# Low parts of the rotated queries and keys in retention: made by GpSimd in place of the vector engine

## The reference

```python
q = rotary(q.reshape(B, S, H, RET_QK), positions)
k = rotary(k.reshape(B, S, H, RET_QK), positions) * (RET_QK ** -0.5)
def step(R, chunk):
    qc, kc, vc = chunk
    inner = jnp.einsum('bhqk,bhkd->bhqd', jnp.einsum('bhqd,bhkd->bhqk', qc, kc) * decay_in[None], vc)
    cross = jnp.einsum('bhqd,bhde->bhqe', qc, R) * xi[None, :, :, None]
    R = R * gamma_c[None, :, None, None] + jnp.einsum('bhkd,bhke->bhde', kc * zeta[None, :, :, None], vc)
    return R, inner + cross
```

## Time and profile before

| | |
|---|---|
| time, median of 3 runs | 1608.7 us (1607.95 to 1609.33) |
| the profiled execution, its own time | 1608.6 us |
| span, first to last instruction | 1606.8 us |
| mean granted PE clock | 0.995 |

### The profile page before, as it was taken

How to read it: one execution, slowest core, us unless ns; L and a number is a source line. 1 busy time by engine, 2 the same in 40 slices (tenths; PEclk the granted TensorE clock), 3 DMA queues, 4 the chain that set the end, 5 groups by cost and what they waited for, 6 DMA issues and landing times. The chain is left out here.

```text
span 1606.8 us, 20289 instructions
## 1 busy us (share of the span) xinstructions
PE 1565.4 (97%) x7568; PEld 1306.9 (81%) x7568; DVE 960.0 (60%) x1626; ACT 605.1 (38%) x1057; POOL 323.7 (20%) x280
## 2 busy tenths in 40 slices
PE   5999999999999999999999999999999999999998
PEld 4778888888888888788888888887688888888886
DVE  6984444444444448752665666667978775647544
ACT  5443333333333353342343333434544444213111
POOL 2232222333232200200000000025545530000000
PEclk8999999999999999999999999999999999999999
DMA  9133233323333234699364464548977767344332
GB/s 385 41 120 116 105 112 111 111 106 112 110 125 107 92 107 157 263 414 341 122 210 158 167 213 166 175 143 278 322 227 226 252 208 274 113 149 179 136 105 79
DMA packets 142225, 278.70 MB, mean 173 GB/s; under 512 B 11056, under 2 KB 83632, under 8 KB 133552
## 3 DMA queue, kind: packets, MB, share of 16 engines
q1 hardware_dynamic: 125488, 245.09, 43.9%
q10 hardware_dynamic: 12032, 15.54, 2.9%
q0 software_dynamic: 4608, 16.78, 2.6%
HBM read 182.47 MB, written 94.37 MB: 172 GB/s over the span
## 5 line engine op out<-in xcount | busy, mean ns | idle before, releaser
L1586 DVE TENSOR_TENSOR w_form<-w_pair,w_form 128x512 fp32r<-128x512 f32 x150 | 116.3, 777 | 127.2 <-ACT w_form L1218 125.6
L1218 ACT ACTIVATE w_form<-w_pair 128x512 fp32r<-128x512 f32 x150 | 94.6, 632 | 245.2 <-PE p_banks L2100 237.2
L2097 PE MATMUL p_banks<-h_hi,w_form 128*128 128x512 f32 x300 | 116.8, 389 | 1.1 <-DVE w_form L1586 1.1
L2100 PE MATMUL p_banks<-h_hi,w_form 128*128 128x512 f32 x300 | 116.7, 389 | 0.0
L2099 PE MATMUL p_banks<-h_lo,w_form 128*128 128x512 f32 x300 | 116.7, 389 | 0.0
L1290 ACT ACTIVATE prob<-p_banks,neg_max 128x128 f32<-128x128 f32 (+3 forms) x64 | 47.5, 742 | 183.0 <-DVE neg_max L1700 183.0
L529 ACT ACTIVATE w_hi<-w_raw 128x1024 fp32r<-128x1024 f32 (+3 forms) x63 | 53.1, 847 | 135.8 <-PE p_banks L2355 97.9
L2355 PE MATMUL p_banks<-y_hi,w_lo 128*128 128x512 f32 x256 | 99.6, 389 | 0.0
L2354 PE MATMUL p_banks<-y_lo,w_hi 128*128 128x512 f32 x256 | 99.6, 389 | 0.0
L2353 PE MATMUL p_banks<-y_hi,w_hi 128*128 128x512 f32 x256 | 99.6, 389 | 0.0
L1062 POOL DMA_DIRECT2D v_ret<-v_stage x32 | 17.7, 554 | 399.2 <-DVE v_stage L1677 399.1
(11 more groups left out here) (318 smaller groups left out, 4313.9 us busy)
## 6 DMA issues: line engine op xcount, KB each, us to landing
w_pair<-in_w_pairs SPq DMA_DIRECT2D x25, 1024.0 KB, 4.8
w_raw<-in_w_dense SPq DMA_DIRECT2D x39, 512.0 KB, 4.7
v_ret<-v_stage POOLq DMA_DIRECT2D x32, 512.0 KB, 3.3
v_chunk<-v_ret SPq DMA_DIRECT2D x32, 512.0 KB, 3.8
merge_t<-act_t SPq DMA_DIRECT2D x48, 256.0 KB, 3.4
act_t<-stage SPq DMA_DIRECT2D x40, 256.0 KB, 2.0
act_t<-stage_late SPq DMA_DIRECT2D x40, 256.0 KB, 2.0
ada<-in_w_ada SPq DMA_DIRECT2D x4, 2048.0 KB, 23.8
```

The costliest lines, as they stand in the source:

```text
L1218: self.nc.scalar.activation(self.form[f % FORM_SLOTS][:, 0, :], self.form_source(f), ACT.Copy).then_inc(self.form_hi, 1)
L1586: nc.vector.tensor_tensor(self.form[f % FORM_SLOTS][:, 1, :], self.form_source(f), self.form[f % FORM_SLOTS][:, 0, :].bitcast(F32), ALU.su ...
L2097: self.nc.tensor.matmul(out, w_hi[:, cut], x_hi[:, q, :], start=fresh and q == 0, stop=False, skip_group_check=True)
L2100: last = self.nc.tensor.matmul(out, w_lo[:, cut], x_hi[:, q, :], start=False, stop=q == KD // 2 - 1, skip_group_check=True)
```

## The change

`low_qk` is issued on POOL in place of DVE: the same subtraction, of the same operands into the same place, behind the same wait for ACT's high part, and counted in the same semaphore. On DVE the three calls go. On POOL, `low_qk(n)` stands directly behind the rotation of chunk n for n from 2 on; `low_qk(0)` comes at g = 64 and `low_qk(1)` at g = 66, both behind the rotations of chunks 0 and 1. Buffers and all other work stay.

```diff
--- before.py
+++ after.py
@@ -1029,11 +1029,16 @@
             if g == STEPS - 2:
                 for n in range(2):
                     self.rotate_chunk(pool, n)
+            if g == STEPS:
+                self.low_qk(pool, 0)
+            if g == STEPS + 2:
+                self.low_qk(pool, 1)
         for n in range(2, CHUNK_STEPS):
             if n == 9:
                 for unit in range(units, FILL_UNITS):
                     self.store_fill(pool, unit)
             self.rotate_chunk(pool, n)
+            self.low_qk(pool, n)
 
     def rotate_chunk(self, pool, n):
 
@@ -1332,9 +1337,9 @@
             act.wait_ge(self.out_done, n - 1)
         self.nc.scalar.activation(self.qk[:, n % 2, 0:4, :], self.qk_raw[n % 3][:, 0:4, :], ACT.Copy).then_inc(self.qk_hi_ready, 1)
 
-    def low_qk(self, dve, n):
-        dve.wait_ge(self.qk_hi_ready, n + 1)
-        self.nc.vector.tensor_tensor(self.qk[:, n % 2, 4:8, :], self.qk_raw[n % 3][:, 0:4, :],
+    def low_qk(self, pool, n):
+        pool.wait_ge(self.qk_hi_ready, n + 1)
+        self.nc.gpsimd.tensor_tensor(self.qk[:, n % 2, 4:8, :], self.qk_raw[n % 3][:, 0:4, :],
                                      self.qk[:, n % 2, 0:4, :].bitcast(F32), ALU.subtract).then_inc(self.qk_lo_ready, 1)
 
     def high_chunk(self, act, n):
@@ -1735,11 +1740,8 @@
             while parts < self.parts_used(g - 1):
                 self.lower_weight(dve, R_V + V_PARTS + parts)
                 parts += 1
-            if g == STEPS - 1:
-                self.low_qk(dve, 0)
             if g == STEPS + 1:
                 self.low_chunk(dve, 0)
-                self.low_qk(dve, 1)
 
     def merge_unit(self, dve, unit):
 
@@ -1824,8 +1826,6 @@
                 dve.wait_ge(self.yr_stored[s], 16 * (n // 2))
             nc.vector.tensor_tensor(self.y_ret[:, s, :, :], p[:, 0, :].rearrange("p (a n) -> p a n", n=P),
                                     self.gate_chunk[:, n % 3, :, :], ALU.mult).then_inc(self.yr_done, 1)
-            if n + 2 < CHUNK_STEPS:
-                self.low_qk(dve, n + 2)
             if n == len(FILL_LATE) - 1:
                 for unit in range(FILL_UNITS - 2, FILL_UNITS):
                     self.lower_fill(dve, unit)
```

## The result

| | before | after |
|---|---|---|
| time, median (lowest to highest) of 20 runs each | 1606.95 us (1605.45 to 1609.33) | 1610.62 us (1609.25 to 1612.90) |
| ratio, 95% interval | | 1.0023 [1.0017, 1.0030] |
| span of the profiled execution | 1606.8 us | 1609.0 us |

The change costs 3.7 us (interval 2.7 to 4.8, the ratio's ends times 1607). The forecast was 1614.2, +5.6 on the profiled execution; 1610.62 lies in the range. The three runs known when the forecast was made had a median 1.75 us above that of the 20, so part of its distance from the result lies in its starting point.

A forecast was written before the change was run, and what follows sets the result against it. The prediction took PE, busy 97% of the span, as the bound, with DVE mattering only where PE waits for it. Terms 2.0 - 1.6 + 3.0 + 1.4 + 0.8 = +5.6 on 1608.6 gave 1614.2 us, range 1609.5 to 1618.5.

The forecast's parts named there:

- the first rival: Chunks 4 and 5: POOL doesn't get between two successive DVE instructions; each loses 0.35; +3.3 us, 1611.9; chance 0.18.
- Term 1: Head of retention: PE stands still for POOL's subtraction of chunk 0, queued behind two rotations; +2.0 us.
- Term 2: Chunks 0 and 3, where DVE was late on its own: the splits end earlier, 1.0 and 0.6; -1.6 us.
- so I see no cover: Head: nothing later hides PE's 2.0 us stop, as all hangs on PE or a load behind it.
- Term 3: Chunks 4 and 5: POOL's subtraction and a rotation product take turns with DVE's splits, 1.5 us each; +3.0 us.
- neither is stretched: Kernel before: POOL's rotation runs while DVE reads PSUM, so neither engine slows the other; no size given.
- Term 4: Chunks 6 to 8: chunk 9's rotation, behind two stores, ends late, delaying ACT and chunk 8's statistics; +1.4 us.
- Term 5: Later chunks: one POOL turn delays w_lo ahead of the statistics, 0.64 in chunk 15, 0.2 in chunk 22; +0.8 us.
- The clock: PE's slow stretch from 1108.4 to 1111.8 us: one lost and one gained cancel; 0, between -1.6 and +3.2 us.
- The Trainium skill's other rule: DVE and POOL sharing SBUF: DVE instructions with one SBUF input don't contend; no size given.
- The second: From 1085 to 1165 us: DVE's relief reaches PE, waits and slow clock go; -6.3 us, 1602.3; chance 0.07.
- The third: POOL's chain per chunk, 8.6 against 7.5 us, becomes the bound; some ten chunks late; +5 on top, 1619; chance 0.13.

The follow-up runs named there:

- Experiment 2: The changed kernel with chunk 0's subtraction put between the head's two rotations on POOL: 1608.23 us, 1.0012 of the kernel before.
- experiment 9: The kernel before with only chunk 0's subtraction moved to POOL, between the head's two rotations: 1605.26 us, ratio 0.9986.
- the repeat: The kernel before, timed and profiled once more without an edit: 1606.63 us, ratio 1.0002.
- Experiment 4: The changed kernel with the rotations of chunks 7, 8 and 9 held until DVE's splits are made: 1609.11 us, 1.0017 of the kernel before.
- experiment 5: The kernel before with only the subtractions of chunks 6, 7 and 8 moved to POOL: 1612.42 us, ratio 1.0033.
- 6: The kernel before with only the subtractions of chunks 2 and 5 moved to POOL: 1606.73 us, ratio 0.9998.
- 7: The kernel before with only the subtractions of chunks 0 and 1 moved to POOL, behind both head rotations: 1608.24 us, ratio 1.0004.
- 8: The changed kernel, all 32 subtractions on POOL but several re-placed among the rotations, chunk 9's rotation held: 1605.90 us, 0.9994 of the kernel before.
- 10: The kernel before with the subtractions of chunks 0 to 3 moved to POOL, chunk 0's between the head's rotations: 1605.37 us, ratio 0.9985.
- experiment 3: The changed kernel with each subtraction from chunk 3 on behind the next chunk's rotation: 1608.61 us, 1.0017 of the kernel before.

## Why the prediction was right, and where it was off

The direction and the mechanism hold; the sum was 5.6 us for 3.7 measured, and 4.7 by the waits of the two profiles. Of the 3.6 us between 1614.2 and 1610.62, 1.65 is the execution that the forecast started from (1608.6 for a median of 1606.95), and 1.9 the sum. By the time alone the first rival, at +3.3, comes nearer than the forecast; the trace is what decides for the forecast. By its own steps:

- **Term 1, the head: 1.67 for 2.0**. The subtraction took 1.26 us and the rotation ended a little sooner than taken. Experiment 2 shows that the order costs it: without it 1.8 us are gone.
- **Term 2, chunks 0 and 3: 2.1 gained for 1.6.** Chunk 0 gave 1.85 for 1.0, and here a step failed: "Everything later hangs on PE's fills, on the load of chunk 2 behind them, or on PE itself, so I see no cover" took the load as fixed to PE. It hangs on DVE as well: with low_qk(0) gone, y_full, SP's loads and so the rotation of chunk 2 come sooner, worth 0.8 us in experiment 9. Chunk 3 gave 0.25 for 0.6: the 1.21 us wait of the earlier trace rows was 0.75 in the repeat.
- **Term 3, chunks 4 and 5: 2.7 for 3.0.** The y_lo pair took 3.71 us where 3.4 was forecast, as POOL's subtraction itself held the first one; PE's wait went from 0.20 to 1.52. Experiment 4 shows that the rotation's turns make most of it, experiment 5 that these places lose it by themselves. Such turns were not new: in the kernel before POOL's products take 2.11 us at 1143.50 and 1.76 at 1151.91, behind DVE's splits, so "neither is stretched" does not hold throughout.
- **Term 4, chunks 6 to 8: 1.7 for 1.4, in another place, so that its size is luck.** The pair of chunk 6 was forecast 0.2 late and the statistics of chunk 8 1.4. It was chunk 6 itself: the stores take 1.13 us, the rotation of chunk 9 still meets the second y_lo, and the pair takes 3.86 for the 2.36 of the earlier trace rows. Chunk 8 lost 0.16. The step took the rotation to begin behind the second y_lo; it began ahead of it, and the turns of term 3 applied to this pair too.
- **Term 5: 0.73 for 0.8**; chunk 15's w_lo took 1.72 us for 1.23, and PE waited 1.16 for 0.68.
- **The clock: 0.** The stretch at half clock of the earlier trace rows is missing in the profile after, where two new long waits brought none. But the mean granted clock is 0.9954 over the 20 executions after and 0.9955 over 33 of the kernel before, so nothing of it is left in the medians. The price was about right: a granted clock of 0.53 means that nearly all of the 3.4 us, not half, ran at the 1.2 GHz level, and in three experiments without the stretch (6, 7 and 9) chunk 2 comes 1.4 us sooner against chunk 1.

The first rival (no turn of POOL between two DVE instructions) is refuted by the pair of chunk 4. By the rule of the Trainium skill (SBUF — State Buffer, Who interferes with whom) that whichever issues first holds the pair for a whole instruction, this was to be expected, and the trace agrees: POOL's products take 2.27 and 2.15 us for 1.3 where each waits for a y_lo of 1.2. The Trainium skill's other rule there, on DVE instructions with one SBUF input, carries a condition that the prediction left out, outside the 2-port perf modes; no number of the prediction rests on it. The second, relief of DVE that reaches PE, failed in its mechanism at chunk 4 (y_lo began behind ACT's y_hi, after 0.58 us of waiting). DVE was not saturated there either, at 65.0 of 80 us. But relief of DVE did reach PE in one place, at the head, by a path that the rival did not name. The third, POOL as the bound, is refuted: POOL waits for ACT ahead of 31 of its 32 subtractions, 52.9 us in all.

What is open: the profiles' waits give 4.7 us and the medians 3.7; 4.7 is still inside the interval of 2.7 to 4.8. In experiments 6, 8, 9 and 10 too the time is 1 to 2.5 us lower than the same reckoning against the repeat gives. The half-clock stretch, which is in the two profiles of the kernel before and in none of these between 1080 and 1170 us, may be part of it; that is not shown.

## What to carry to other kernels

An instruction that is moved takes its place in the new engine's queue, and what stands behind it there moves too: here the moved 1.3 us cost 1.67 us at the head and little elsewhere, and the rotation that it pushed into DVE's splits cost most of the 4.2 us lost behind chunks 4 to 6. So look for the one or two places where the old engine's delay reaches the critical engine, follow that path through DMA queues as well, and move only those: one instruction of 32 gained 0.14% (0.05 to 0.23, of which the waits explain 0.04), all of them lost 0.23%. When two engines take turns at whole instructions, the order and start of each matter more than the busy share of either.

## What the runs showed of the hardware that was not expected

- **The half-speed stretches of PE's clock don't follow from the waits.** With PE waiting 1.46 and 0.96 us in chunks 1 and 2, nearly as in the kernel before, the profile of experiment 5 has no such stretch there, and one from 1156.96 to 1160.38 us behind the wait of 2.02; the change, with the same wait of 2.02, has none, and experiment 3 has one from 1088.19 behind the 1.67 us at the head, where the change has none. One profiled execution can't tell what the clock costs a kernel; the mean granted clock over its runs says more, and from kernel to kernel it went from 0.9942 to 0.9960 here, 2.9 us of 1607.
- **A DVE instruction of 1.28 us set how fast a load landed 10 us later**: the 128 KB tables of chunks 2 and 3 took 5.2 us from issue to landing in the kernel before and 4.9 in its repeat (three loads there), and 4.3 in experiment 9, which moves that instruction alone. (In the change it is 3.5, but there PE is 1.67 us late as well, which delays the issue of these loads.)
